# Expert stage: token rows gathered in four 1 KB pieces and turned by VectorE blocks instead of TensorE transposes

## The chip, the cores and the metric

One core of a Trainium2 chip runs the whole program. The metric is the device time of one launch in microseconds. The kernel before took 3232.83 us (median of 3 runs, 3229.73 to 3238.44).

## What is computed

Two transformer blocks over 1024 tokens of width 1024, all in fp32. The first has attention, a long convolution and a gated MLP; the second has three kinds of attention and then a mixture of experts. Only the experts are touched by the change:

```python
g_logits = x @ w_rg + b_rg                       # 4 groups
grp = argmax(g_logits)
e_logits = (x @ w_re[grp]) + b_re                # 8 experts in the group
top_val, top_idx = lax.top_k(e_logits, 2)        # 2 of 32 experts for each token
gate = softmax(top_val) * p_grp
# for each of a token's two experts e:
y_e = (silu(x @ w_gate[e]) * (x @ w_up[e])) @ w_down[e]    # 1024 -> 256 -> 1024
out[token] = sum over its two experts of gate * y_e
```

There are 1024 x 2 = 2048 pairs of token and expert.

## The kernel before

The program keeps every engine's instructions in one long stream for each engine, stage after stage. The last stages are the routing (`pe_route`, `dve_choose`, `dve_place`), the experts (`*_experts`) and the final sum and norm (`*_final`).

**Placement.** There are 32 blocks of 128 slots (NBLK), one for each expert, 4096 slots in all. Block i holds the tokens of expert i in its first slots. Slots 64 to 127 of a block form a second side with weight buffers of its own (GUEST_GU, GUEST_DN): they are first filled with a copy of the block's own weights, and an indirect load over them brings another expert's weights only where an expert has more than 128 tokens; its indices are out of bounds otherwise, and rows out of bounds are skipped. `dve_place` works out, per pair, block and slot; TensorE sums one-hot products into a table `slots` (slot in the partition, block in the column, L2677) that holds the token's number, 0 for an empty slot (constant "tok"); `widx` (L2851) holds the weight rows of the guest.

**The expert loop.** Iterations i = 0 to 33; each engine's order within one is written by hand:

- POOL (`pool_experts`, L2902 on): gathers the rows of block i+2 (L2906, 128 rows of 4 KB from the DRAM tensor `xtok` into XG, one instruction, on the software queue q0), then the guest gate/up load of block i (L2893, waits for VectorE's copy `cg`), then the guest down load of block i-1 (L2899).
- SP: on the hardware queue q1 loads the own weights of a later block (L2879, 2 MB; L2882, 1 MB) and stores the block's result (L3063, 512 KB to `yslot`).
- TensorE (`pe_experts`): `pe_ex(i)` (L2929, 8 transposes of 128x128 from XG to two PSUM banks), `pe_eht(i-2)` (L2952, 2 transposes), `pe_egu(i-1)` (L2943, 32 matmuls of 512 columns, both sides), `pe_edn(i-2)` (L2965, 16 matmuls). `pe_egu(i)` waits for XB(i), for the own weights and for the guest load ("bg", i).
- VectorE (`dve_experts`): half of block i's turned rows from PSUM to XB (L3026), hidden values of i-2 (L3031), the copy of the own gate/up weights into the guest buffer (L3013, 128x4096, gives "cg"), the product for i-1 (L3042), half of the result of i-2 (L3047); in eight iterations also a scaling (L3021).
- ScalarE: the other half of the turned rows (L2996), the copy of the down weights (L2988), silu (L3002), the other half of the result (L3007).

XG, XB, and both guest buffers are double. The stage ends with gathers of `yslot` (L3110) and the final norm.

Of the kernel before, what the change touches and what calls it, by code (L numbers as in the profile page):

```python
# [5 lines left out]
U32 = mybir.dt.uint32  # L6
ALU = mybir.AluOpType
ACT = mybir.ActivationFunctionType
# [112 lines left out]
def build(nc, X, out):  # L121
# [2462 lines left out]
    didx16 = room(16)  # L2584
    FS = marks["end"]
# [9 lines left out]
    didx = [didx16.bitcast(U32)[:, 8 * q:8 * q + 8] for q in range(2)]  # L2595
    g1f, g2f = g1.rearrange("p j u -> p (j u)"), g2.rearrange("p j u -> p (j u)")
# [59 lines left out]
    def pe_route():  # L2656
# [29 lines left out]
        held[b] = [("widx",)]  # L2686

# [95 lines left out]
    def dve_place():  # L2783
        V.wait_ge(*(yield ("cumrank",)))
# [62 lines left out]
        vt.tensor_copy(slots.bitcast(U32), bk(bank["slots"], NBLK)).then_inc(*V.step(("slots",)))  # L2847
# [3 lines left out]
        vt.tensor_copy(widx.bitcast(U32), be).then_inc(*V.step(("widx",)))  # L2851
        vt.tensor_tensor(picked, slot_e, con("bidx").rearrange("p (u e) -> p u e", u=1).broadcast_to([128, 16, 32]), MUL).then_inc(*V.step())
# [49 lines left out]
    def pool_rows(i):  # L2902
        if i > 1:
            G.wait_ge(*(yield ("ex", i - 2, 1)))
        GD.ready()
        gt.indirect_dma_start(sb(XG + i % 2 * 1024, 1024), None, x_d, by_row(slots.bitcast(U32)[:, i:i + 1])).then_inc(*GD.turn(("xg", i)))  # L2906

    def pool_experts():
        G.wait_ge(*(yield ("xk", 7, 1)))
        G.wait_ge(*(yield ("slots",)))  # L2910
        for j in range(8):
            G.wait_ge(*(yield ("xd", j)))
        yield from pool_rows(0)
        yield from pool_rows(1)
        G.wait_ge(*(yield ("widx",)))
        for i in range(NBLK + 1):
            if i + 2 < NBLK:
                yield from pool_rows(i + 2)
            if i < NBLK:
                yield from pool_guest_gu(i)  # L2920
            if i:
                yield from pool_guest_dn(i - 1)

    def pe_ex(i):
        for h2 in range(2):
            yield from claim(h2)
            P.wait_ge(*(yield ("xg", i)))
            for k in range(4):
                ins = turn(bk(h2, 128, off=k * 128), sb(XG + i % 2 * 1024 + (4 * h2 + k) * 128, 128), ident)  # L2929
            ins.then_inc(*P.step(("ex", i, h2)))  # L2930
            held[h2] = [("xb", i, h2)]

    def pe_egu(i):
        b = 2 + i % 2
        yield from claim(b)
        P.wait_ge(*(yield ("xb", i, 0)))
        P.wait_ge(*(yield ("xb", i, 1)))
# [32 lines left out]
    def pe_experts():  # L2970
        for i in range(NBLK + 2):
            if i < NBLK:
                yield from pe_ex(i)
            if i >= 2:
                yield from pe_eht(i - 2)
            if 1 <= i <= NBLK:
                yield from pe_egu(i - 1)
            if i >= 2:
                yield from pe_edn(i - 2)
# [10 lines left out]
    def act_experts():  # L2990
        for i in range(NBLK + 2):
            if i < NBLK:
                if i > 1:
                    A.wait_ge(*(yield ("egu", i - 2)))
                A.wait_ge(*(yield ("ex", i, 1)))
                st.activation(sb(XB + i % 2 * 1024 + 512, 512), bk(1), ACT.Copy).then_inc(*A.step(("xb", i, 1)))  # L2996
# [18 lines left out]
    def dve_experts():  # L3015
        for j in range(8):
            V.wait_ge(*(yield ("xd", j)))
        for i in range(NBLK + 2):
# [3 lines left out]
            if i < NBLK:  # L3022
                if i > 1:
                    V.wait_ge(*(yield ("egu", i - 2)))
                V.wait_ge(*(yield ("ex", i, 0)))
                vt.tensor_copy(sb(XB + i % 2 * 1024, 512), bk(0)).then_inc(*V.step(("xb", i, 0)))  # L3026
# [244 lines left out]
def _constants():  # L3271
# [25 lines left out]
    put("tok", 128 * np.arange(8)[None] + i[:, None])  # L3297
# [48 lines left out]
def _layout(I):  # L3346
# [19 lines left out]
    for n, s in (("qna", "qn_a"), ("kna", "kn_a"), ("qnd", "qn_d"), ("knd", "kn_d")):  # L3366
# [43 lines left out]
        wgu=np.stack([I["w_expert_gate_2"][0], I["w_expert_up_2"][0]], axis=2).reshape(32, 8, 128, 512).transpose(0, 2, 1, 3).reshape(4096, 4096),  # L3410
# [20 lines left out]
```

## Time and profile before

| | |
|---|---|
| median of 3 runs | 3232.83 us |
| the profiled execution | 3227.49 us, its span 3225.9 us |
| granted TensorE clock over the span | 0.982 of full |
| TensorE busy | 3055.8 us (95%) |
| VectorE, ScalarE, POOL busy | 1601.0, 938.6, 245.8 us |
| chain that ended last | TensorE 85%, ScalarE 7%, VectorE 6% |
| expert loop, from the first row gather to the last result stored | 2773.3 to 3167 us of the span |

A share of busy time says little about what a stage waits for: each of the stages before the routing is untouched by the change, and the expert loop has to be read by itself. "DMA share" is the mean busy share of the core's 16 DMA engines; q0 is the queue of the POOL engine's indirect transfers, q1 that of SP.

### The profile page before, as it was taken

The numbers are of one execution on the slowest core, as the hardware profiler recorded it, in microseconds if no ns is written. First come the engines' busy times: TensorE is split into PE (matmuls) and PEld (weight loads), VectorE is DVE, ScalarE is ACT, GpSimd is POOL, SyncE is SP. The second block draws the span as 40 slices with busy tenths as digits, with TensorE's granted clock in tenths as the row PEclk, the third lists the DMA queues.
The fourth block names the chain that finished last, engine by engine and source line by source line (L and its number), as shares of the span: only waits on it lengthen the run. The fifth ranks groups of instructions, "written<-read, shape, count | busy, mean of one in ns | idle before, by whom it ended". The sixth has DMA issues, their size and how long they took to land.

```text
span 3225.9 us, 30362 instructions
## 1 busy us (share of the span) xinstructions
PE 3055.8 (95%) x12214; PEld 1629.6 (51%) x12214; DVE 1601.0 (50%) x2659; ACT 938.6 (29%) x1766; POOL 245.8 (8%) x174
## 2 busy tenths in 40 slices
PE   7999999899999999999999998899999998699997
PEld 3456557566664444444444454675846643333332
DVE  6467677466653555544564422312366525443334
ACT  4112462477772100000000001212335613222223
POOL 1000231000000000000000000000000000234431
PEclk9999999999999999999999999999999999799999
DMA  6113213000003211111121020000120013599994
GB/s 244 52 65 131 79 53 118 1 1 1 1 27 132 93 49 39 51 41 40 43 90 36 27 94 27 20 30 20 50 69 1 27 52 119 185 358 358 360 336 177
DMA packets 61512, 298.19 MB, mean 92 GB/s; under 512 B 14826, under 2 KB 21242, under 8 KB 39868
## 3 DMA queue, kind: packets, MB, share of 16 engines
q1 hardware_dynamic: 45244, 271.05, 23.2%
q0 software_dynamic: 16128, 25.21, 2.2%
q8 instruction: 96, 1.57, 0.2%
q14 instruction: 44, 0.36, 0.0%
HBM read 365.32 MB, written 31.55 MB: 123 GB/s over the span
## 4 chain that ended last, share of the span: by engine, by line
PE 85%; ACT 7%; DVE 6%; issue 1%; DMA 1%; another core or an unknown queue 0%; POOL 0%; SPq 0%; DVEq 0%; ACTq 0%; POOLq 0%
PE ps L1385 16%; PE ps L1512 8%; PE ps L2943 7%; PE ps L1687 6%; PE ps L906 5%; PE ps L2965 3%; PE ps L1309 3%; PE ps L2448 3%; PE ps L1689 3%; PE ps L1059 3%; PE ps L763 3%; PE ps L909 2%; PE ps L1087 2%; PE ps L2206 2%; ACT arena L1138 2%; PE ps L1071 1%
## 5 line engine op out<-in xcount | busy, mean ns | idle before, releaser
L1385 PE MATMUL ps<-arena 128*128 128x512 f32 x1232 | 529.6, 592 | 1.0 <-DVE arena L1416 1.0
L1385 PEld LDWEIGHTS ps<-arena 128*128 128x128 f32 x1232 | 233.3, 189 | 297.3 <-issue 287.4
L1512 PE MATMUL ps<-arena 128*128 128x512 f32 x616 | 264.5, 592 | 0.0
L2943 PE MATMUL ps<-arena 128*64 128x512 f32 x1024 | 229.6, 600 | 5.2 <-DMA arena<-in_wgu_dram,arena 5.2
L1687 PE MATMUL ps<-arena 128*128 128x512 f32 x480 | 209.5, 597 | 0.0
L1193 DVE TENSOR_SCALAR_CACHE_REDUCE arena<-ps 128x1280 f32<-128x1280 f32 x96 | 139.3, 1489 | 111.9 <-PE ps L1059 111.9
L1512 PEld LDWEIGHTS ps<-arena 128*128 128x128 f32 x616 | 116.6, 189 | 147.8 <-issue 143.7
L906 PE MATMUL ps<-arena 128*128 128x512 f32 (+1 forms) x432 | 173.6, 555 | 0.7 <-DVE arena L389 0.7
L2109 POOL COPY arena<-arena 64x512 f32<-64x512 f32 x8 | 5.6, 695 | 1887.1 <-DVE arena L2102 1886.8
L1687 PEld LDWEIGHTS ps<-arena 128*128 128x128 f32 x480 | 91.0, 191 | 114.1 <-issue 114.1
L2943 PEld LDWEIGHTS ps<-arena 128*64 128x64 f32 x1024 | 73.8, 137 | 138.2 <-issue 138.2
L1704 DVE COPY arena<-ps 128x512 f32<-128x512 f32 (+2 forms) x31 | 16.6, 537 | 248.0 <-PE ps L1687 158.2
L1151 ACT ACTIVATE arena<-arena 128x1280 f32<-128x1280 f32 x96 | 129.6, 1354 | 8.2 <-DVE arena L1193 8.2
L1059 PE MATMUL ps<-arena 64*128 64x512 f32 (+1 forms) x576 | 121.0, 552 | 6.8 <-DVE arena L1193 3.1
L906 PEld LDWEIGHTS ps<-arena 128*128 128x128 f32 x432 | 82.1, 191 | 84.7 <-issue 81.4
L1071 PE MATMUL ps<-arena 128*128 128x128 f32 x640 | 100.3, 286 | 24.4 <-ACT arena L1138 21.0
L2906 POOL DMA_INDIRECT arena<-xtok,arena x32 | 82.3, 2571 | 539.6 <-DVE arena L2851 363.4
L1138 ACT ACTIVATE arena<-ps 128x512 f32<-128x512 f32 (+1 forms) x192 | 93.7, 522 | 87.0 <-PE ps L1071 84.4
L2965 PE MATMUL ps<-arena 128*64 128x512 f32 x512 | 115.7, 592 | 0.5 <-DVE arena L3031 0.5
L2448 PE MATMUL ps<-arena 128*128 128x512 f32 x256 | 111.0, 592 | 0.7 <-DVE arena L2414 0.7
L1309 PE MATMUL ps<-arena 128*128 128x512 f32 x256 | 110.4, 592 | 0.0
L1689 PE MATMUL ps<-arena 128*128 128x256 f32 (+1 forms) x512 | 104.5, 364 | 0.0
(432 smaller groups left out, 4553.8 us busy)
## 6 DMA issues: line engine op xcount, KB each, us to landing
arena<-in_wgu_dram SPq DMA_DIRECT2D x32, 2048.0 KB, 8.4
arena<-in_wed_dram SPq DMA_DIRECT2D x32, 1024.0 KB
arena<-in_wmod_dram SPq DMA_DIRECT2D x24, 1024.0 KB, 4.9
arena<-in_wup_dram SPq DMA_DIRECT2D x22, 1024.0 KB, 4.8
arena<-in_wout_dram SPq DMA_DIRECT2D x16, 1024.0 KB, 4.9
yslot<-arena SPq DMA_DIRECT2D x32, 512.0 KB, 9.6
arena<-in_wdn_dram SPq DMA_DIRECT2D x16, 704.0 KB, 4.1
arena<-in_w2b_dram SPq DMA_DIRECT2D x9, 1024.0 KB, 4.9
```

Of the source, the lines that this page charges most:

```text
L906: ins = mm(bk(b, size), sb(wat(n) + k * 256 + col, 128), x, k == 0, k == 7)
L1059: ins = mm(bk(3 * j + c // 512, n), sb(q + h * 1024 + qt * 128, 128, 64 * j, 64 * j + 64), sb(key + c, n, 64 * j, 64 * j + 64), True, True)
L1138: st.activation(probt(i, j, g * 512, n), bk(bank[("turn", i, j, g)], n), ACT.Copy).then_inc(*A.step(("pt", i, j, g)))
L1193: vt.tensor_scalar(prob(i, j), scores(j), -SCALE, None, MUL, ALU.min, accum_out=stat(i, f"bias{j}")).then_inc(*V.step(("cmax", i, j)))
L1309: ins = mm(bk(b), sb(wat(n) + k * 256 + f % 2 * 128, 128), sb(YT + k * 1024 + tc * 512, 512), k == 0, k == 7)
L1385: ins = mm(bk(b), left[:, k], right[:, k], k == 0, k == 3)
L1512: ins = mm(bk(b), sb(left + k * 128, 128), right(k), k == 0, k == 10)
L1687: ins = mm(bk(b), sb(w, 128), sb(x + tile * 512, 512), k == 0, k == 7)
L1689: ins = mm(bk(b, size), views[ty](x, tile), sb(w, size), k == 0, k == 7)
L2448: ins = mm(bk(b), sb(wat(n) + k * 256 + f % 2 * 128, 128), sb(OF + k * 1024 + tc * 512, 512), k == 0, k == 7)
L2943: ins = mm(bk(b, 512, *rows), sb(XB + i % 2 * 1024 + k * 128 + 64 * side, 64), sb(w + k * 512, 512), k == 0, k == 7)
L2965: ins = mm(bk(6 + h2, 512, *rows), sb(HB + 512 + i % 2 * 256 + k * 128 + 64 * side, 64), sb(w + k * 1024 + h2 * 512, 512), k == 0, k == 1)
```

## The change

- `slots` stays in fp32. The constant "tok" becomes 4 x token - 8192, so that an empty slot reads 0 and a full one a negative number.
- New: `quarter` (partition // 32 + 8192, four small VectorE operations, two of them a rounding), `every` (one VectorE copy, 128x512) ahead of everything in `dve_place`; four matmuls of 32 columns in `pe_route` that spread slot 32a+s to partitions s, 32+s, 64+s, 96+s; two VectorE operations that make `sidx` from them: 4 x token + quarter, or 8192 and more for an empty slot, which the bounds check skips.
- A block's rows are gathered by four indirect transfers of 128 pieces of 1 KB (partition 32b+s gets quarter b of the row of slot 32a+s) in place of one of 128 rows of 4 KB; POOL waits for `sidx` instead of `slots`, and puts the transfers in another order around the guest loads.
- `pe_ex` and its two PSUM copies (on VectorE and ScalarE) go; one VectorE transpose of 32x32 blocks, 128x1024, makes XB from XG.
- The rows of the gate/up weights are laid out in DRAM to fit, on the host.

```diff
+    sidx, quarter, every = room(4 * NBLK), room(1), room(512)
+    x_q = x_d.rearrange("t (b c) -> (t b) c", b=4)
...
+        b = next(banks)
+        yield from claim(b)
+        P.wait_ge(*(yield ("slots",)))
+        for a in range(4):
+            ins = mm(bk(b, NBLK, off=NBLK * a), every[:, 128 * a:128 * a + 128], slots, True, True)
+        bank["spread"] = b
+        ins.then_inc(*P.step(("spread",)))
+        held[b] = [("sidx",)]
...
     def dve_place():
+        vt.tensor_scalar(quarter, con("pidx"), 1 / 32, -31 / 64, MUL, ADD).then_inc(*V.step())
+        vt.tensor_copy(every.rearrange("p (a b s) -> p a b s", a=4, b=4),
+                       ident.rearrange("p (a u s) -> p a u s", a=4, u=1).broadcast_to([128, 4, 4, 32])).then_inc(*V.step(("every",)))
+        dve_round(quarter)
+        vt.tensor_scalar(quarter, quarter, 8192.0, None, ADD).then_inc(*V.step())
         V.wait_ge(*(yield ("cumrank",)))
...
-        vt.tensor_copy(slots.bitcast(U32), bk(bank["slots"], NBLK)).then_inc(*V.step(("slots",)))
+        vt.tensor_copy(slots, bk(bank["slots"], NBLK)).then_inc(*V.step(("slots",)))
...
         vt.tensor_copy(widx.bitcast(U32), be).then_inc(*V.step(("widx",)))
+        V.wait_ge(*(yield ("spread",)))
+        vt.tensor_scalar(sidx, bk(bank["spread"], 4 * NBLK), quarter, None, ADD).then_inc(*V.step())
+        vdone()
+        vt.tensor_copy(sidx.bitcast(U32), sidx).then_inc(*V.step(("sidx",)))
...
-    def pool_rows(i):
+    def pool_rows(i, quarters):
         if i > 1:
-            G.wait_ge(*(yield ("ex", i - 2, 1)))
-        GD.ready()
-        gt.indirect_dma_start(sb(XG + i % 2 * 1024, 1024), None, x_d, by_row(slots.bitcast(U32)[:, i:i + 1])).then_inc(*GD.turn(("xg", i)))
+            G.wait_ge(*(yield ("xb", i - 2)))
+        for a in quarters:
+            GD.ready()
+            gt.indirect_dma_start(sb(XG + i % 2 * 1024 + a * 256, 256), None, x_q, by_row(sidx.bitcast(U32)[:, NBLK * a + i:NBLK * a + i + 1]),
+                                  bounds_check=4095, oob_is_err=False).then_inc(*GD.turn(("xg", i, a)))
...
-        yield from pool_rows(0)
-        yield from pool_rows(1)
         G.wait_ge(*(yield ("widx",)))
+        G.wait_ge(*(yield ("sidx",)))
+        yield from pool_rows(0, (0, 1, 2, 3))
+        yield from pool_guest_gu(0)
+        yield from pool_rows(1, (0, 1, 2, 3))
         for i in range(NBLK + 1):
             if i + 2 < NBLK:
-                yield from pool_rows(i + 2)
-            if i < NBLK:
+                yield from pool_rows(i + 2, (0, 1))
+            if 0 < i < NBLK:
                 yield from pool_guest_gu(i)
+            if i + 2 < NBLK:
+                yield from pool_rows(i + 2, (2, 3))
             if i:
                 yield from pool_guest_dn(i - 1)
...
-        P.wait_ge(*(yield ("xb", i, 0)))
-        P.wait_ge(*(yield ("xb", i, 1)))
+        P.wait_ge(*(yield ("xb", i)))
...
                 if i > 1:
                     V.wait_ge(*(yield ("egu", i - 2)))
-                V.wait_ge(*(yield ("ex", i, 0)))
-                vt.tensor_copy(sb(XB + i % 2 * 1024, 512), bk(0)).then_inc(*V.step(("xb", i, 0)))
+                for a in range(4):
+                    V.wait_ge(*(yield ("xg", i, a)))
+                vt.transpose(sb(XB + i % 2 * 1024, 1024).rearrange("p (k a s) -> p a k s", k=8, a=4),
+                             sb(XG + i % 2 * 1024, 1024).rearrange("p (a k s) -> p a k s", k=8, a=4)).then_inc(*V.step(("xb", i)))
...
-    put("tok", 128 * np.arange(8)[None] + i[:, None])
+    put("tok", 4 * (128 * np.arange(8)[None] + i[:, None]) - 8192)
...
-        wgu=np.stack([I["w_expert_gate_2"][0], I["w_expert_up_2"][0]], axis=2).reshape(32, 8, 128, 512).transpose(0, 2, 1, 3).reshape(4096, 4096),
+        wgu=np.stack([I["w_expert_gate_2"][0], I["w_expert_up_2"][0]], axis=2).reshape(32, 4, 8, 32, 512).transpose(0, 1, 3, 2, 4).reshape(4096, 4096),
```

## Rows read from the trace of the kernel before

**Rows 1.** The page's busy times: engine, us, share, instructions.
```profile
PE 3055.8 (95%) x12214; PEld 1629.6 (51%) x12214; DVE 1601.0 (50%) x2659; ACT 938.6 (29%) x1766; POOL 245.8 (8%) x174
```

**Rows 2.** The chain of waits: start us, us, what; its first blocks and last one.
```profile
2773.30 4.80 DMA arena<-xtok,arena
...
2783.41 3.80 DMA arena<-in_wgu_dram,arena
...
2787.35 9.36 PE ps L2943 x32
...
2798.14 7.03 PE ps L2943 x32
...
2809.85 7.03 PE ps L2943 x32
2816.89 3.43 PE ps L2965 x16
2820.32 1.02 PE ps L2929 x8
...
3148.23 0.37 PE ps L2952 x2
3148.60 7.03 PE ps L2943 x32
3155.63 3.43 PE ps L2965 x16
```

**Rows 3.** Stretches: us, busy of PE, PEld, DVE, ACT, POOL, PEclk, DMA share, GB/s.
```profile
2787.00:2789.00 2.00, 1.65 (x4) 0.59 (x6) 0.00 (x0) 0.00 (x0) 1.39 (x3) 0.50 0.45 104
2820.93:2832.64 11.71, 11.71 (x60) 4.64 (x59) 5.00 (x6) 3.40 (x5) 4.71 (x3) 1.00 1.01 362
```

**Rows 4.** Timeline of VectorE in one block: start us, us, what, [idle before].
```profile
2818.65 0.69 DVE L3047 COPY arena<-ps 128x512 f32<-128x512 f32 x1 [0.87 <-PE ps L2965]
...
2820.95 0.69 DVE L3026 COPY arena<-ps 128x512 f32<-128x512 f32 x1 [1.00 <-PE ps L2929]
2821.60 0.42 DVE L3031 COPY arena<-ps 128x256 f32<-128x256 f32 x1
2821.94 2.28 DVE L3013 COPY arena<-arena 128x4096 f32<-128x4096 f32 x1
```

**Rows 5.** VectorE by line, 2763 to 2767 us: one-pass operation, 1024 elements, both sides SBUF.
```profile
L2835 DVE TENSOR_TENSOR arena<-arena 128x1024 f32<-128x1024 f32 x2 | 2.4, 1218 | 0.0
```

**Rows 6.** Timeline of POOL: the first two gathers, then one block's three issues.
```profile
2773.30 1.59 POOL L2906 DMA_INDIRECT arena<-xtok,arena  x1 [363.42 <-DVE arena L2851]
2775.19 0.94 POOL L2906 DMA_INDIRECT arena<-xtok,arena  x1 [0.30 <-issue]
...
2821.62 2.73 POOL L2906 DMA_INDIRECT arena<-xtok,arena  x1 [6.03 <-PE ps L2952]
2825.02 0.99 POOL L2893 DMA_INDIRECT arena<-in_wgu_dram,arena  x1 [0.67 <-issue]
2826.31 0.99 POOL L2899 DMA_INDIRECT arena<-in_wed_dram,arena  x1 [0.31 <-issue]
```

**Rows 7.** POOL by line, 2773 to 3160 us: xcount, busy us, mean ns, idle before.
```profile
L2906 POOL DMA_INDIRECT arena<-xtok,arena x32 | 82.3, 2571 | 539.6 <-DVE arena L2851 363.4 <-PE ps L2952 162.8 <-PE ps L2929 12.8
```

**Rows 8.** TensorE by line, 2765 to 2773 us: the 16 matmuls of 32 columns.
```profile
L2677 PE MATMUL ps<-arena 128*128 128x32 f32 x32 | 7.0, 401 | 9.6 <-DVE arena L2835 9.6
```

**Rows 9.** Timeline of VectorE in the routing: a wait, the slots, the guests' rows.
```profile
2755.66 0.19 DVE L2786 TENSOR_SCALAR arena<-ps 128x32 f32<-128x32 f32 x1 [0.93 <-PE ps L2670]
...
2772.26 0.19 DVE L2847 CAST arena<-ps 128x32 uint32<-128x32 f32 x1 [4.62 <-PE ps L2677]
```

**Rows 10.** Line L2893, the guest gate/up load, all 32: from issue to landing.
```profile
DMA to landing us min/median/max: 6.1/6.7/7.4
```

**Rows 11.** DMA queues, 2859.6 to 2862.8 us: packets, MB, share.
```profile
q1 hardware_dynamic: 155, 0.94, 96.9%
```

**Rows 12.** DMA queues, 2863.4 to 2865.4 us.
```profile
q0 software_dynamic: 338, 0.45, 61.1%
q1 hardware_dynamic: 58, 0.32, 60.2%
```

**Rows 13.** DMA queues, 3176 to 3185 us: gathers of 4 KB rows alone.
```profile
DMA packets 976, 3.55 MB, mean 395 GB/s; under 512 B 109, under 2 KB 109, under 8 KB 976
```

**Rows 14.** DMA queues, 2344.5 to 2350.3 us: a load of 1,056-byte rows alone.
```profile
DMA packets 1950, 2.04 MB, mean 352 GB/s; under 512 B 16, under 2 KB 1950, under 8 KB 1950
```

**Rows 15.** DMA queues, 2786.5 to 2787.8 us: the first guest load, all rows skipped.
```profile
q0 software_dynamic: 144, 0.00, 4.9%
```

More of the change, by code:

```diff
@@ L2900, in pool_guest_dn @@
                               bounds_check=4095, oob_is_err=False).then_inc(*GD.turn(("bd", i)))
-    def pool_rows(i):
+    def pool_rows(i, quarters):
         if i > 1:
-            G.wait_ge(*(yield ("ex", i - 2, 1)))
-        GD.ready()
-        gt.indirect_dma_start(sb(XG + i % 2 * 1024, 1024), None, x_d, by_row(slots.bitcast(U32)[:, i:i + 1])).then_inc(*GD.turn(("xg", i)))
+            G.wait_ge(*(yield ("xb", i - 2)))
[3 more added lines that the diff above has]
+                                  bounds_check=4095, oob_is_err=False).then_inc(*GD.turn(("xg", i, a)))
     def pool_experts():
         G.wait_ge(*(yield ("xk", 7, 1)))
-        G.wait_ge(*(yield ("slots",)))
         for j in range(8):
             G.wait_ge(*(yield ("xd", j)))
-        yield from pool_rows(0)
-        yield from pool_rows(1)
         G.wait_ge(*(yield ("widx",)))
+        G.wait_ge(*(yield ("sidx",)))
+        yield from pool_rows(0, (0, 1, 2, 3))
+        yield from pool_guest_gu(0)
+        yield from pool_rows(1, (0, 1, 2, 3))
         for i in range(NBLK + 1):
             if i + 2 < NBLK:
-                yield from pool_rows(i + 2)
-            if i < NBLK:
+                yield from pool_rows(i + 2, (0, 1))
+            if 0 < i < NBLK:
                 yield from pool_guest_gu(i)
+            if i + 2 < NBLK:
+                yield from pool_rows(i + 2, (2, 3))
             if i:
                 yield from pool_guest_dn(i - 1)
[L2924 to L2931, printed above, removed]
     def pe_egu(i):
@@ L2971, in pe_experts @@
         for i in range(NBLK + 2):
-            if i < NBLK:
-                yield from pe_ex(i)
             if i >= 2:
@@ L2991, in act_experts @@
         for i in range(NBLK + 2):
[L2992 to L2996, printed above, removed]
             if 1 <= i <= NBLK:
```

## The prediction

> **What bounds the kernel now.** I read the page's busy times first: TensorE is busy for 95% of the span [rows 1], and the change takes work off it, in the expert loop alone. So the second view is the chain of waits over that loop [rows 2]. It is a strict pattern: down matmuls 3.43 us, the transposes of the gathered rows 1.02 us, two short transposes, gate/up matmuls 7.03 us, from one start at 2809.85 us to the last at 3148.60 us. TensorE waits for nothing in between; the period is 11.71 us. The stretch of one period [rows 3] shows the second thing: the DMA engines are busy too, 362 GB/s at a share of 1.01. TensorE sets the pace, and the transfers just keep up. The start is different: chain pieces of 4.80 and 3.80 us are DMA landings [rows 2], one after the other.
>
> **TensorE, per block.** Removed: the 8 transposes, 1.02 us on the path. The last iteration has none of them and shows the period that would remain: 0.37 + 7.03 + 3.43 = 10.83 us [rows 2]. That is 0.88 us less than 11.71 (the two short transposes then hide less). This is the floor.
>
> **VectorE and ScalarE.** The two PSUM copies go (0.69 us on VectorE [rows 4], about as much on ScalarE, which is far from full). The block transpose has no row. Nearest is a one-source-rate operation over 1024 elements, 1.22 us [rows 5]; lower bound the 2.28 us for 4096 elements [rows 4] scaled to 1024, 0.6; upper bound twice the first, 2.4. I take 1.22, the row nearest in elements and in operands. VectorE goes from 5.00 us a period [rows 3] to 5.5 of 10.8: no bound. It also no longer needs TensorE: it may start when the result copy ends, 0.98 us before TensorE's iteration starts (2819.34 against 2820.32 [rows 2, 4]), and ends at +0.24 us.
>
> **POOL, per block.** Six issues in place of three. A free issue takes 0.94 to 0.99 us and 0.30 to the next [rows 6]. The mean of the row gathers is 2.57 us [rows 7], but the one that starts at 2821.62 ends at 2824.35, 0.13 us after VectorE's big copy (2821.94 to 2824.22 [rows 4]): it stands still under the copy. The copy comes once a block, so I charge that stall once. From TensorE's iteration start: gather 0 from 0.4 to 3.3 (the copy now ends at 3.1), gather 1 3.6 to 4.6, guest load issued at 4.9, gathers 2 and 3 to 8.5, down load to 9.8. It fits into 10.8 with 1 us to spare. Twelve semaphore waits more for the transfers in flight (they take their turns among 16) wait for landings two blocks old: free.
>
> **The guest load decides.** It moves nothing (all rows skipped), but gate/up of block i waits for it. Before, it is issued at +4.70 (2825.02) and lands 6.7 us later [rows 6, 10], at +11.4, needed at +12.95: 1.5 us early. Now it is issued at +4.9 and needed at 10.83 + 0.37 = +11.2. With the same 6.7 us it lands at +11.6, 0.4 late, which makes the period 11.23. But what lies ahead of it shrinks. While q1 had work, q0 moved nothing [rows 11], and once q1 ran dry q0 moved its 0.5 MB [rows 12]: the queues are served about in order of arrival. Ahead of it in q0 are now two gathers of at most 0.26 MB instead of 0.52. At 395 GB/s for 4 KB rows [rows 13] and 352 for 1,056-byte ones [rows 14] that is 0.75 us instead of 1.33: landing at +11.0, just in time. The landings vary by 0.6 to 0.7 us [rows 10], so some come late: I take 10.93 us for the period (ends 10.83 and 11.4).
>
> **Bytes.** 2048 pairs fill half of 4096 slots, so the loop moves 3.93 MB a block on the average instead of 4.19; 256 more skipped pieces cost little: 144 packets took 4.9% of 1.3 us [rows 15], 0.06 us, so 0.12. DMA work falls by 1.33 - 0.75 - 0.12, some 0.45 us a period (0.26 MB at 285 to 395 GB/s gives 0.92 to 0.66).
>
> The trace has 395 GB/s out of HBM over 9 us [rows 13], so I do not take the loop's 362 for a ceiling. The Trainium skill (DMA: Bandwidth & Descriptors, Where 436 GB/s comes from) says that loads from HBM are bound at about 358 GB/s for a core. By that, as an estimate, 3.93 MB give a period of 10.98 us, 1.5 us more over the loop than mine; the gathers' rate speaks against it here.
>
> **The routing.** New work ahead of the wait for the counts: five VectorE operations, about 1.2 us (0.2 each, the 512-element copy 0.4), of which 0.93 lie in a wait that is there [rows 9]: +0.3. The spread: 8 passes at 7.0/32 = 0.22 us [rows 8], 1.75 us, with two small VectorE operations and the handovers: gathers start at about 2775.8 instead of 2773.3, +2.5 us.
>
> **The start of the loop.** Four gathers instead of one before block 0 can be turned: the fourth is issued by 2781.1 and has landed by 2783.1; transpose to 2784.3, copy to 2786.6, guest load issued 2786.9, landed 1.1 us after its end: gate/up of block 0 at 2789.1 instead of 2787.35. It runs on a cold clock as before (0.50 granted, 1.2 GHz [rows 3], 9.36 us instead of 7.03 [rows 2]) and ends at 2798.5. Then POOL's queue is in the way: between the guest loads of blocks 0 and 1 stand ten gathers (four of block 1, four of 2, two of 3), 10 x 1.25 us and one stall under a copy: issued about 2802.8 instead of 2787.65. The own load of block 3, issued at 2798.5, lies ahead in the DMA engines until about 2805. So gate/up of block 1 starts at about 2806.5 instead of 2798.14, after 8 us of idle TensorE, likely with the clock at its lower level again: 9.4 us. Block 2 starts at about 2820 instead of 2809.85: **+10 us** for the start as a whole (bounds +3, if POOL's issues overlap better, and +13). Cover that is gone: before, block 1's guest load went out 10 us ahead of need.
>
> **Sum.** From 2809.85 to 3148.60 are 338.75 us. Now 29 periods x 10.93 = 317.0: -21.8. With the start, +10: **-12 us**. The tail is unchanged. Profiled execution 3227.49 (span 3225.9), so about 3215.5; the median of the runs shown is 5 us above that execution, so I say 3221 for the median.
>
> **Rivals.**
> - *A late guest load each block.* Its landing time stays at 6.9 us or the transfers do not get cheaper: 4.9 + 6.9 - 0.37 = 11.4 us a period, 29 x 11.4 = 330.6, -8 + 10 = +2: 3235. For it: 1.5 us of margin before, and the change takes 0.88 of it by speed alone. Against: half the bytes.
> - *POOL becomes the bound (the slower end).* If each row gather takes 2.57 us wherever it stands [rows 7]: 4 x 2.57 + 1.04 + 0.99 + 6 x 0.30 = 14.1 us a period, 29 x 2.4 = +70, +10: 3313. It decides from 1.5 us per issue on (6 x 1.8 = 10.8). Against: 0.94 and 0.99 where no copy runs [rows 6]. A milder form is a second stall of 1.7 us a block, which only just goes over: 11.9 a period, +15: 3248.
> - *Small pieces choke the transfers.* The Trainium skill (DMA: Bandwidth & Descriptors, Measured) warns that transfers under 64 KB are descriptor-dominated; the gathers shrink from 512 to 128 KB. On the rows, 1,056-byte packets run at 352 GB/s when many are queued [rows 14]; for this to cost, 0.26 MB would have to take longer than 1.8 us. It would end in the same place as the first rival.
> - *The start costs little:* +3, period 10.83: 314.1 - 338.75 + 3 = -22: 3211.
> - *The empty slots are not skipped:* 8192 and more is over the bound 4095, so no; it would be the first rival.
>
> **Chances.** Forecast 0.52, late guest load or dearer transfers 0.27, POOL 0.11, cheap start 0.10. 0.3% is 9.7 us, about what a measurement can tell from no change: faster means below 3223. My forecast lies only 2 us under that, so of its 0.52 I count 0.37 as faster. Faster 0.47, same 0.40, slower 0.13. The range takes in the cheap start with the runs' spread of some 4 us and the late guest load: 3206 to 3240.
>
> **What would show it.** Right: chain pieces 0.37, 7.03, 3.43 without L2929, a period of 10.8 to 11.1; POOL with one long gather and three of 1 us; a VectorE transpose of 1.2 us; block 2's gate/up at about 2820. Wrong: chain pieces "DMA in_wgu" or POOL in every block (late guest load, POOL), POOL busy over 10 us a period, a first period start before 2813, or a DMA share under 0.9.

## The result, and the profile after

The changed kernel takes **3251.37 us** (median of 4 runs, 3249.51 to 3252.67) against 3232.11 for the kernel before beside it: a ratio of 1.0051, 95% interval 1.0032 to 1.0069. It is slower by about 19 us (the two medians alone give 1.0060), where I had forecast 12 us less and a range of 3206 to 3240. The profiled execution is one of 3249.51 us.

The page of the changed kernel: the span, busy times, DMA queues, the chain's shares, and three of its groups of instructions (two matmul lines of the experts and the row gathers).

```profile
span 3248.2 us, 30137 instructions
PE 3039.5 (94%) x11966; PEld 1609.0 (50%) x11966; DVE 1617.2 (50%) x2666; ACT 919.3 (28%) x1734; POOL 343.9 (11%) x270
q1 hardware_dynamic: 45244, 271.05, 23.2%
q0 software_dynamic: 17664, 16.86, 1.6%
PE 77%; DVE 7%; ACT 7%; DMA 4%; issue 3%; POOL 1%; another core or an unknown queue 0%; POOLq 0%; DVEq 0%; SPq 0%; ACTq 0%
L2957 PE MATMUL ps<-arena 128*64 128x512 f32 x1024 | 232.1, 605 | 26.1 <-DMA arena<-in_wgu_dram,arena 26.1
L2926 POOL DMA_INDIRECT arena<-xtok,arena x128 | 181.6, 1419 | 465.5 <-DVE arena L2871 366.6
L2979 PE MATMUL ps<-arena 128*64 128x512 f32 x512 | 116.6, 594 | 22.1 <-DMA arena<-in_wed_dram,arena 19.1
```

TensorE's gate/up matmuls (L2957) now stand idle 26.1 us for the guest gate/up load, its down matmuls (L2979) 22.1 us, 19.1 of them for the guest down load. Both loads carry nothing here: all their rows are skipped. Of before, the chain had the first only ahead of block 0 [rows 2], and the second nowhere.

Most of the 26.1 us lie at the start of the loop, ahead of blocks 0 and 1:

```profile
2794.07 10.09 PE L2957 MATMUL ps<-arena 128*64 128x512 f32 x32 [15.15 <-DMA arena<-in_wgu_dram,arena]
2813.50 8.91 PE L2957 MATMUL ps<-arena 128*64 128x512 f32 x32 [7.91 <-DMA arena<-in_wgu_dram,arena]
```

Behind them, in the 29 periods up to block 31, TensorE waits for the gate/up load twice, 3.0 us in all, and for the down load fifteen times, 19.1 us in all. In the steady loop it is the down load that is late. Who waited for its line, L2918 (us, times):

```profile
  PE ps L2979: 19.1, 15
```

The chain of waits, two neighbouring blocks (columns: start us, us, what):

```profile
2835.26 10.68 DMA arena<-in_wed_dram,arena
2845.94 0.14 issue
2846.08 3.65 PE ps L2979 x16
2849.73 0.37 PE ps L2966 x2
2850.10 7.05 PE ps L2957 x32
...
2866.40 10.11 DMA arena<-in_wgu_dram,arena
2876.51 0.14 issue
2876.65 3.62 PE ps L2957 x15
```

The matmul pieces are those of the forecast (0.37, 7.05 us; the down matmuls take 3.65 us behind a wait and 3.43 without one); between them stand landings of 10.68 us (down load) and 10.11 us (gate/up load). Wherever the chain of these periods shows a late down load, it landed 9.1 to 10.9 us after its issue. Before, the guest gate/up load landed after 6.1 to 7.4 us [rows 10], the guest down load after 2.1 to 6.2 us, with a median of 5.5. The gate/up matmuls of blocks 2 to 31 start from 2826.1 to 3169.3 us, 29 periods of 10.83 to 15.8 us with a mean of **11.83** (the expectations below round it to 11.84); before, a constant 11.71 (the last one shorter), which makes a mean of 11.68.

GpSimd in one block (start us, us, what):

```profile
2851.27 2.60 POOL L2926 DMA_INDIRECT arena<-xtok,arena  x1 [3.37 <-DVE arena L3040]
2854.18 1.00 POOL L2926 DMA_INDIRECT arena<-xtok,arena  x1 [0.30 <-issue]
2855.48 0.99 POOL L2912 DMA_INDIRECT arena<-in_wgu_dram,arena  x1 [0.30 <-issue]
2856.77 1.00 POOL L2926 DMA_INDIRECT arena<-xtok,arena  x1 [0.30 <-issue]
2858.08 1.00 POOL L2926 DMA_INDIRECT arena<-xtok,arena  x1 [0.30 <-issue]
2859.38 1.00 POOL L2918 DMA_INDIRECT arena<-in_wed_dram,arena  x1 [0.30 <-issue]
```

One issue stretched under VectorE's copy, five of 1.00 us: as worked out, and GpSimd is done 9.1 us after it began. But it begins later than worked out. Counted from the start of TensorE's two short transposes (2849.73 here), the guest gate/up load is issued at +5.6 us in the median block instead of +4.9, and the guest down load at +9.5; before, the down load was issued at +6.0, counted from the start of the eight transposes.

VectorE's block transpose, the new operation (line, operation, shapes, count, busy us, mean ns, idle before):

```profile
L3034 DVE STREAM_TRANSPOSE arena<-arena 128x1024 f32<-128x1024 f32 x32 | 39.6, 1237 | 21.5 <-DMA arena<-xtok,arena 21.5
```

**Where the 22.3 us between the two spans lie.** 4.3 lie ahead of the routing's matmuls, which start at 2769.5 instead of 2765.2. I take them for drift: of the change only a few small VectorE operations stand there, and the first gather of kernels that are alike up to it starts anywhere from 2775.2 to 2780.6. From there to the first gather 11.04 instead of 8.09: +2.95. First gather to block 2's gate/up 45.6 instead of 36.5: +9.1. The 29 periods: 343.2 instead of 338.75, +4.4. The tail: +1.5.

### The profile page after: what moved, and what is told of

Same layout as the page of the kernel before. It is cut to its first block, busy times and chain, and to the rows that moved or that the text cites. A ratio compares the mean times of both kernels' runs of the same rounds, so it can differ in the third digit from the quotient of the medians.

```text
span 3248.2 us, 30137 instructions
## 1 busy us (share of the span) xinstructions
PE 3039.5 (94%) x11966; PEld 1609.0 (50%) x11966; DVE 1617.2 (50%) x2666; ACT 919.3 (28%) x1734; POOL 343.9 (11%) x270
## 3 DMA queue, kind: packets, MB, share of 16 engines
q0 software_dynamic: 17664, 16.86, 1.6%
## 4 chain that ended last, share of the span: by engine, by line
PE 77%; DVE 7%; ACT 7%; DMA 4%; issue 3%; POOL 1%; another core or an unknown queue 0%; POOLq 0%; DVEq 0%; SPq 0%; ACTq 0%
PE ps L1385 16%; PE ps L1512 8%; PE ps L1687 6%; PE ps L906 5%; PE ps L1309 3%; PE ps L2448 3%; PE ps L1689 3%; DMA arena<-in_wed_dram,arena 3%; PE ps L1059 3%; PE ps L763 3%; PE ps L909 2%; PE ps L2957 2%; PE ps L2979 2%; PE ps L1087 2%; ACT arena L1138 2%
## 5 line engine op out<-in xcount | busy, mean ns | idle before, releaser
L2957 PE MATMUL ps<-arena 128*64 128x512 f32 x1024 | 232.1, 605 | 26.1 <-DMA arena<-in_wgu_dram,arena 26.1
L2926 POOL DMA_INDIRECT arena<-xtok,arena x128 | 181.6, 1419 | 465.5 <-DVE arena L2871 366.6
L2957 PEld LDWEIGHTS ps<-arena 128*64 128x64 f32 x1024 | 75.6, 139 | 159.9 <-issue 159.9
L2979 PE MATMUL ps<-arena 128*64 128x512 f32 x512 | 116.6, 594 | 22.1 <-DMA arena<-in_wed_dram,arena 19.1
```

Of the source, the lines that this page charges most:

```text
L2926: gt.indirect_dma_start(sb(XG + i % 2 * 1024 + a * 256, 256), None, x_q, by_row(sidx.bitcast(U32)[:, NBLK * a + i:NBLK * a + i + 1]), boun ...
L2957: ins = mm(bk(b, 512, *rows), sb(XB + i % 2 * 1024 + k * 128 + 64 * side, 64), sb(w + k * 512, 512), k == 0, k == 7)
L2979: ins = mm(bk(6 + h2, 512, *rows), sb(HB + 512 + i % 2 * 256 + k * 128 + 64 * side, 64), sb(w + k * 1024 + h2 * 512, 512), k == 0, k == 1)
```

## The experiments

All times are medians; the ratio is to the kernel before on the same chip, and the quotient of the two medians differs from it by up to 0.0015; the mean period is that of blocks 2 to 31 in the profiled run.

| kernel | us | ratio (95%) | mean period |
|---|---|---|---|
| changed | 3251.4 | 1.0051 (1.0032 to 1.0069) | 11.83 |
| no_guest_loads | 3206.1 | 0.9916 (0.9895 to 0.9937) | 10.84 |
| one_gather | 3279.2 | 1.0125 (1.0091 to 1.0159) | 13.85 |
| one_gather_hold | 3288.4 | 1.0155 (1.0122 to 1.0188) | 13.71 |
| loads_first_loop | 3237.5 | 1.0011 (0.9993 to 1.0028) | 11.52 |
| after_small_own | 3232.8 | 0.9994 (0.9984 to 1.0005) | 11.27 |
| after_empty_fetched | 3249.3 | 1.0048 (1.0031 to 1.0064) | 11.96 |
| early_copy | 3209.9 | 0.9917 (0.9889 to 0.9945) | 10.84 |
| early_copy_start | 3216.0 | 0.9941 (0.9920 to 0.9962) | 10.85 |
| before_skipped_more | 3239.1 | 1.0020 (1.0002 to 1.0038) | 11.88 |
| before_empty_skipped | 3235.8 | 1.0002 (0.9987 to 1.0018) | 11.68 |
| before_early_copy | 3229.2 | 0.9987 (0.9977 to 0.9996) | 11.68 |
| before_four_pieces | 3348.4 | 1.0344 (1.0312 to 1.0376) | 15.34 |
| before_four_skipped | 3360.5 | 1.0391 (1.0366 to 1.0417) | 15.88 |
| before_four_split | 3249.8 | 1.0039 (1.0020 to 1.0057) | 12.16 |

### 1. Without the guest loads

```
-        yield from pool_guest_gu(0)
...
-            if 0 < i < NBLK:
-                yield from pool_guest_gu(i)
...
-            if i:
-                yield from pool_guest_dn(i - 1)
```

> The changed kernel with both guest loads of every block left out (with these inputs they skip every row; their place is taken by VectorE's and ScalarE's copies, on which TensorE now waits). Turns theory: the last transfers of queue q0 land late because every piece, skipped ones too, takes a turn with q1's packets, and the guest loads are what TensorE waits for: without them the period falls from 11.84 to 10.83 us, 29 periods give back some 29 us against the changed kernel, the start a little more: about 0.5% faster than before, near 3215 us. Rival, transfers at their ceiling: the small pieces cost the DMA engines more than the empty slots save, the own weights come late, and the period stays at 11.8: +15 us against before. Rival, POOL or VectorE too slow: the period stays above 11.5.

Both guest loads are left out (the copies stay, and with these inputs nothing is loaded by them). Measured: 3206.1 us, and a period of 10.83 to 10.84 in every block. The chain (start us, us, what):

```profile
2885.77 0.37 PE ps L2959 x2
2886.14 7.03 PE ps L2950 x32
2893.17 3.44 PE ps L2972 x16
```

So the forecast's floor is real, and the loss in the periods goes with the two loads that move nothing. The start is cheap too: block 2 at 2810.2.

### 2. One gather of whole rows, and guest loads first

```
-        for a in quarters:
+        if quarters[0] == 0:
...
-            gt.indirect_dma_start(sb(XG + i % 2 * 1024 + a * 256, 256), None, x_q, ...
+            gt.indirect_dma_start(sb(XG + i % 2 * 1024, 1024), None, x_d, ...
```

> The changed kernel with one gather of whole 4 KB rows for each block in place of the four (empty slots still skipped), and the same VectorE transpose; the rows then do not lie in quarters, so what is computed from them is another product of the same size. Turns theory: q0 holds 24 pieces a block for each engine instead of 48, the guest loads land as early as before, period 10.83 to 10.95 us, and the start loses only 3 to 5 us: 3212 us, 0.6% faster than before. Rival, the VectorE transpose or the order of the loop is what costs: period as in the changed kernel, 11.8, 3245 us.

The rows lie in another layout than the block transposes want. The expectation has the empty slots still skipped; in effect they are not. The one column of indices that it uses holds slots 0 to 31 four times over, which are nearly always full, and q0 moves 25.11 MB in all, against 16.86 in the changed kernel and 25.21 in the one before. So it compares four gathers of the full slots with one gather of as many bytes as before. Measured: 3279.2 us, slower still, where I had expected 3212. Fewer issues do not cure it. Here it is the guest gate/up load that is late: TensorE waits for it in 14 of the 29 periods, 54.6 us in all, though it is issued at +4.3 us. GpSimd here issues all the rows, then both guest loads. In the next kernel they come in the reverse order:

```
         for i in range(NBLK + 1):
+            if i:
+                yield from pool_guest_dn(i - 1)
+            if 0 < i < NBLK:
+                yield from pool_guest_gu(i)
             if i + 2 < NBLK:
-                yield from pool_rows(i + 2, (0, 1))
+                yield from pool_rows(i + 2, (0, 1, 2, 3))
```

> The changed kernel with POOL's order in the loop turned round: guest down load, guest gate/up load, then the four gathers of block i+2. Nothing else. Turns theory: the guest loads no longer have the block's 16 to 32 pieces an engine ahead of them, they land 4 us or more earlier, TensorE does not wait, period 10.85 to 11.1; the start stays as in the changed kernel (+12 us against before): 3222 to 3230 us. Rival, transfers at their ceiling: the same bytes and pieces, so no change from the changed kernel, 3250 us.

Measured: 3237.5 us, between the expectation (3222 to 3230) and its rival (3250). The down load, now issued first, at +3.3 us, is waited for in no period; the gate/up load in five, 12.0 us in all. Across the three kernels the period falls with what stands ahead of the guest loads: all rows 13.85 us, half of them 11.83, none 11.52. The first of the three also differs in the form and the bytes of its gather, so the order alone is shown only by the other two.

> The kernel before with one more indirect transfer in each block, 128 pieces that are all out of bounds and skipped, issued just ahead of the guest gate/up load. It moves nothing. Turns theory: 8 more pieces in each engine's q0, each waiting for a packet of q1 of up to 16 KB (0.4 to 0.7 us), so the guest load lands 3 to 5 us later than now, 2 to 3.5 us past the 1.5 us of margin: period 13 to 15 us, 3270 to 3330 us. Rival, order of arrival (the prediction's reading): a skipped piece costs 7 ns, the issue moves 1.3 us, which the margin covers: no change, 3230 to 3235 us.

This one puts a gather of 128 pieces that are all skipped ahead of the guest gate/up load in the kernel before. Measured: 3239.1 us, a period of 11.71 but for two blocks (15.67 and 13.41, with one guest landing of 11.1 us). The turns theory, which had 13 to 15 us a period, fell here: in nearly every block the 128 skipped pieces cost nothing, as the rival had it (the median landing is 5.8 us, from an issue 0.9 us later). The one late block shows that the kernel before stands close to an edge.

### 3. What the two queues do

Ahead of the next experiments I read the DMA queues in stretches (packets, MB, share of the 16 engines). The kernel before, 2857 to 2862.5 us, then 2863.5 to 2866:

```profile
q1 hardware_dynamic: 219, 1.82, 95.9%
...
q1 hardware_dynamic: 54, 0.36, 53.1%
q0 software_dynamic: 380, 0.47, 51.3%
```

The gather issued from 2856.75 on (its issue on GpSimd ends at 2859.48) gets nothing up to 2862.5, with two own loads and the store of the results issued before it; then q1 is nearly dry and q0 does most of its block's work, 380 packets, in 2.5 us. The next own gate/up load is issued at 2863.76, and when its large packets move, from about 2866 on, q0 is almost through. The changed kernel, inside the landing of 10.11 us, 2872 to 2874 us, then 2874 to 2876:

```profile
q1 hardware_dynamic: 49, 0.80, 98.1%
q0 software_dynamic: 39, 0.00, 1.2%
...
q1 hardware_dynamic: 56, 0.59, 89.1%
q0 software_dynamic: 168, 0.00, 4.9%
```

In the first stretch q1 is at its 2 MB load with packets of 16 KB (0.80 MB in 49), and q0's packets, skipped pieces without bytes, go between them nearly one for one: 39 in 2 us, where 380 took 2.5 us above. From this I took it that taking turns with large packets makes the 10 us of an empty load. In the second stretch q0 moves three packets for each of q1's. The Trainium skill (DMA: Bandwidth & Descriptors, Queues, rings and completion order) says that each engine goes round-robin between its queues, packet by packet; the first stretch agrees (39 to 49), the stretch of before in which q0 had nothing does not. The profile adds up 16 engines, so no stretch shows the turns of one of them.

Another reading is the order of issue. SyncE issues the own gate/up load at 2868.01 and GpSimd the guest down load at 2870.30, behind it; before, the down load was issued at 2861.44, ahead of the own load at 2863.76.

I first took it that the own load issued too early catches q0's tail, and held it back:

```
                 S.wait_ge(*(yield ("egu", i - 1)))
+                S.wait_ge(*(yield ("bg", i)))
                 sp_own_gu(i + 2)
```

> The kernel with one gather of 4 KB rows and VectorE's transposes, with one wait added on SyncE: it does not issue the own gate/up load of block i+2 until the guest gate/up weights of block i have landed. Theory (the last skipped pieces of the other queue are caught behind 16 KB packets of the next own load when that load is issued before they are done): the landing of 12 to 14 us disappears (none over 9), the periods of 15 to 19 us too, and the mean falls from 13.9 to 11.5 or less; the time 3205 to 3245. Rival (the guest loads are late whatever is queued behind them, since the skipped pieces themselves take the time): landings stay at 12 to 14 us, now with the own load late behind them, mean 14 to 16, the time 3280 to 3340.

Measured: 3288.4 us, and the expectation fell. The guest loads still land after 11.5 and 12.7 us (medians; 7.8 and 6.6 without the wait), because the held load is now always issued with the next block's gathers. 2983 to 2987 us:

```profile
q1 hardware_dynamic: 84, 1.38, 80.8%
q0 software_dynamic: 74, 0.30, 19.0%
```

Again nearly one for one, 74 to 84, with 16 KB (1.38 MB in 84) on the other side. Holding the own load does not help. Against the theory stands the kernel without the wait, one_gather, inside a landing of 12.31 us, 2990 to 2995 us:

```profile
q1 hardware_dynamic: 158, 1.97, 97.3%
q0 software_dynamic: 16, 0.01, 0.6%
```

This would still be turns if only one or two engines had packets of q0 left, which the sums over 16 engines do not show. If a guest packet waits for one packet of 16 KB, half the packet should mean half the wait. The next test halves it:

```
-        dma.dma_start(out=sb(OWN_GU[i % 3], 4096), in_=X["wgu"][128 * i:128 * i + 128, :]).then_inc(gusem[i % 3], 16)
+        for c in (0, 2048):
+            dma.dma_start(out=sb(OWN_GU[i % 3] + c, 2048), in_=X["wgu"][...]).then_inc(gusem[i % 3], 16)
```

> The changed kernel with one edit on the other queue: each own gate/up load (2 MB) is issued as two loads of 1 MB, so that its packets are 8 KB instead of 16 KB; the bytes, the order on GpSimd and all the waits stay. Theory (on each DMA engine the packets of the two queues go in turn, one and one, so a piece of the guest queue waits for one packet of the own queue, and the wait is the size of that packet): the guest queue drains up to twice as fast beside the gate/up load, the mean period falls from 11.84 to 10.9 to 11.5, the time to 3215 to 3238. Rival 1 (the guest loads are late because the queues are served in order of arrival, or because the engines' work is too much): nothing changes, 3245 to 3256. Rival 2 (the second issue or the smaller packets cost the own load its rate): slower, over 3256.

Measured: 3232.8 us, the mean period 11.27 instead of 11.83, with no change to the bytes or to what is waited for. In its chain a late gate/up load now lands after 7.02 us, and late down loads after 9.0 to 9.9 us instead of 9.1 to 10.9:

```profile
2836.78 7.02 DMA arena<-in_wgu_dram,arena
2843.80 0.14 issue
2843.94 7.11 PE ps L2958 x32
```

The theory's range held this one; both rivals had said 3245 or more. Of the 22.8 us between the two profiled executions the 29 periods give 16.4; block 2 starts at 2820.5 instead of 2826.1, of which 5.3 is drift before the first gather. The edit halves the packet and also makes two transfers of one, and no run parts these.

### 4. TensorE's pace or the traffic

```
-            gt.indirect_dma_start(sb(XG + i % 2 * 1024, 1024), None, x_d, ...
+            gt.indirect_dma_start(sb(XG + i % 2 * 1024 + a * 256, 256), None, x_q, ...   (a = 0 to 3)
```

> The kernel before, with its one gather of 4 KB rows per block replaced by four gathers of 1 KB pieces to the same places; all rows, the empty ones too, are fetched, and the 32 turns stay on TensorE. Theory (TensorE's 11.71 us period leaves the other queue room, and it is only the shorter period that takes it away): period 11.71 in most blocks, a few later ones, the start of the loop 2 to 3 us later for the three more issues on GpSimd, the time 3234 to 3245. Rival (small pieces cost the DMA engines so much that the loop is bound by them): every period over 12, the time over 3245.

> The kernel before with four gathers of 1 KB pieces instead of one of 4 KB rows, empty slots skipped, and TensorE's turns kept: the changed kernel's data movement at the TensorE period of before. With all pieces fetched this came to a mean period of 15.8 and 3348 us. Theory (fetched 1 KB pieces hold the guest queue up, skipped ones hardly): mean period 11.71 to 12.3, some blocks of 13 and over, the time 3233 to 3255. Rival (the number of packets in the guest queue alone decides, whatever they carry, and that is the same as with all pieces fetched): mean period over 14, the time over 3300.

The second has the same edit with the empty slots skipped. Measured: 3348.4 and 3360.5 us. I had expected some 3240 and 3233 to 3255; the rivals won both. Skipping did not help at all. The cause is GpSimd's queue, which I had left out: all four gathers stand ahead of the guest gate/up load. GpSimd in the second (start us, us, what):

```profile
2884.18 1.00 POOL L2909 DMA_INDIRECT arena<-xtok,arena  x1 [0.30 <-issue]
2885.49 1.00 POOL L2909 DMA_INDIRECT arena<-xtok,arena  x1 [0.30 <-issue]
2886.79 0.99 POOL L2909 DMA_INDIRECT arena<-xtok,arena  x1 [0.31 <-issue]
2888.09 1.00 POOL L2895 DMA_INDIRECT arena<-in_wgu_dram,arena  x1 [0.30 <-issue]
2889.39 0.99 POOL L2901 DMA_INDIRECT arena<-in_wed_dram,arena  x1 [0.30 <-issue]
```

Three more issues of 1.30 us put the load 3.9 us later, where [rows 10] and its need left 1.5 us. That alone does not make waits of 5 to 8 us: its late landings are 8.9 to 11.4 us as well. To part this from the traffic, the same kernel with the changed kernel's order on GpSimd:

```
             if i + 2 < NBLK:
-                yield from pool_rows(i + 2)
+                yield from pool_rows(i + 2, (0, 1))
             if i < NBLK:
                 yield from pool_guest_gu(i)
+            if i + 2 < NBLK:
+                yield from pool_rows(i + 2, (2, 3))
```

> The kernel before with four gathers of 1 KB pieces, empty slots skipped, TensorE's turns kept, and now GpSimd's order of the changed kernel (two gathers, guest gate/up load, two gathers, guest down load), so that the guest load is issued 1.3 us later than before instead of 3.9 us. It is the changed kernel but for who transposes. Theory (the shorter TensorE period takes away the room in which the guest queue is served): period 11.71 in most blocks (mean under 12.0), start up to 10 us later, the time 3233 to 3250. Rival (the four-piece traffic and its issues on GpSimd are enough to make the guest loads late): mean period 12.3 or more, the time 3255 or more.

Measured: 3249.8 us, mean period 12.16, between the two ranges (under 12.0 and over 12.3). Even at TensorE's old pace the new traffic makes guest loads late, here the down load:

```profile
2876.15 10.03 DMA arena<-in_wed_dram,arena
2886.18 0.29 issue
2886.47 3.65 PE ps L2972 x16
2890.13 1.03 PE ps L2936 x8
```

So both halves count: the four gathers cost 12.16 - 11.68 = 0.48 us a block, and TensorE's saving of 0.88 then brings only 12.16 - 11.83 = 0.33. The 0.48 is not traffic alone: the down load is here issued some 4 us later than before, behind the gathers on GpSimd, and it lands after 10 us instead of 5.5. Before, it had 7.6 us to spare (issued at 2826.31, landed 6.2 us later at most, needed at 2840.1), which only the two together use up.

> The changed kernel with the empty slots' pieces fetched (from row 0 of the tokens) instead of skipped: four gathers of 1 KB pieces, 512 fetched pieces per block. Theory (each fetched packet of four 1 KB pieces takes 0.24 us against 0.16 us for a 4 KB row, and stands in front of the guest loads): the mean period rises from 11.84 to 13 to 16, the time to 3280 to 3360. Rival (skipping is worth only its 0.25 MB per block of transfer, 0.6 to 1 us of the engines' work): mean period 12.4 to 12.9, the time 3265 to 3280.

Edit: the constant 8192 that sends empty slots over the bound becomes 0, in `quarter` and in "tok". Measured: 3249.3 us, as the changed kernel. Expectation and rival (3265 to 3280) both fell: 8.35 MB more, and nothing to see.

> The kernel before, with nothing changed but that rows of empty slots are skipped by the gathers. It moves about 8 MB less in the loop, with the period set by TensorE at 11.71. Theory (TensorE sets the period and less work for the DMA engines buys nothing at 11.71): 3228 to 3237, within 0.2% of before. Rival (the DMA engines' work is part of the bound already): period 11.4 to 11.6, the time 3222 to 3229. Other rival (skipped pieces hold the queue up, as in the kernel with one gather and VectorE's transposes): several periods of 13 to 15, the time 3240 to 3260.

The reverse, in the kernel before: 3235.8 us, ratio 1.0002, period 11.71 in every block but the last. Skipping is worth nothing either way. So it is not the bytes of the gathers that count; the order on GpSimd (loads_first_loop) and the packets of the other queue (after_small_own) do.

### 5. More room for the guest load

VectorE's copy of the guest gate/up weights, and with it the load, one block earlier, and the guest down load first in GpSimd's order:

```
+        yield from pool_rows(1, (0, 1, 2, 3))
         yield from pool_guest_gu(0)
-        yield from pool_rows(1, (0, 1, 2, 3))
...
+        yield from pool_guest_gu(1)
+        yield from pool_rows(2, (0, 1, 2, 3))
+        for i in range(1, NBLK + 1):
+            yield from pool_guest_dn(i - 1)
+            if i + 2 < NBLK:
+                yield from pool_rows(i + 2, (0, 1, 2, 3))
+            if i + 1 < NBLK:
+                yield from pool_guest_gu(i + 1)
...
-            if i < NBLK:
-                yield from dve_guest_gu(i)
+            if i == 0:
+                yield from dve_guest_gu(0)
...
                 vt.tensor_tensor(h, h, ..., MUL).then_inc(*V.step(("eh", i - 1)))
+            if i + 1 < NBLK:
+                yield from dve_guest_gu(i + 1)
```

> The changed kernel with VectorE's copy of the guest gate/up weights moved one block earlier, and the guest gate/up load issued a whole block ahead of its use: on GpSimd the order per block is guest down load (i-1), the four gathers of rows (i+2), guest gate/up load (i+1). Theory (the guest loads have no slack, the own loads have some 7 us): the guest gate/up weights may now land up to 8 us later than before without TensorE waiting, so the period falls from a mean of 11.84 towards 10.83 with only the down load left to be late now and then (mean 10.9 to 11.3), and the time to 3205 to 3235. Rival 1 (the DMA engines' work per block is itself about 11.8 us with these small pieces): the period stays at 11.6 to 11.9 and the time at 3245 to 3255. Rival 2 (it is the guest down load alone that is late): the period is irregular as before, with waits on the down load of 1 to 4 us, the time 3240 to 3255.

Measured: **3209.9 us**, 0.9917 of the kernel before (0.9889 to 0.9945), with the whole computation, all six issues and both loads in. The period is 10.83 to 10.84 but for one of 10.95. The down load is issued at +3.3 us instead of +9.5, and the gate/up load at +0.9 us for the block after, so both have gained room. With the down load first alone (loads_first_loop) the period was 11.52. The chain, and one period of it (us, busy us of PE, PEld, DVE, ACT, POOL, then the granted clock, DMA share, GB/s):

```profile
2881.11 7.04 PE ps L2956 x32
2888.15 3.43 PE ps L2978 x16
2891.58 0.37 PE ps L2965 x2
```

```profile
3000.40:3011.24 10.84, 10.84 (x53) 3.79 (x52) 4.69 (x6) 2.79 (x4) 7.90 (x7) 1.00 1.00 376
```

TensorE is busy through the period, and the DMA engines are at a share of 1.00 with 376 GB/s: both are full, neither waits. Rival 1 (the small pieces are too much work for the engines) is refuted by the period.

> The kernel before, with only the order of the kernel called early_copy: VectorE's guest gate/up copy and the guest gate/up load one block earlier. TensorE keeps its turns. It tells whether the 25 us that early_copy gained over the kernel before come from the new order alone. Theory (TensorE's 11.71 us of work set the period, and the order only matters once that is gone): period 11.71, the time 3225 to 3240, within 0.3% of before. Rival (the order alone is worth it): period under 11.5, the time under 3222.

The same order in the kernel before: 3229.2 us, 0.9987, period 11.71. The order alone brings 3 us; the change alone costs 19; both together gain 25. TensorE's work was the bound before, and taking it off only shows once the guest loads have room.

> The kernel called early_copy with another order at the start alone: GpSimd issues the guest gate/up load of block 0 after two gathers of block 1 instead of four, and VectorE's copy for block 1 comes after the transpose of block 1, so that it does not stall the issue of block 0's load. Theory (that load is what block 0's gate/up waits for): gate/up of block 0 starts 2 to 3 us earlier, the period stays at 10.83, the time 3205 to 3208. Rival (the loss moves to block 1, whose rows or load then come late): within 1 us of early_copy, 3209 to 3212.

Edit: at the start `pool_rows(1, (0, 1))`, guest load 0, `pool_rows(1, (2, 3))`, and VectorE's copy for block 1 after that block's transpose. Measured: 3216.0 us, 6 more than early_copy. Block 0 does start earlier (2790.0 instead of 2794.9), but block 2 waits for its guest load and starts at 2817.9 instead of 2816.0. The loss moved, as the rival said, and grew beyond its range (3209 to 3212). The profiled execution is the fastest of six, which go up to 3220.9.

## Why the prediction was wrong

- **TensorE's floor, 10.83 us:** right, shown by no_guest_loads and early_copy.
- **VectorE's transpose, 1.22 us:** 1.24 us, the mean of the 32 above. Right.
- **POOL's six issues in 10.8 us, one stall:** right for the sum (9.1 us). But the first gather starts at +1.0 us where TensorE doesn't wait, not at +0.4, and its issue takes 3.0 us: the guest gate/up load is issued at +5.6 us instead of +4.9.
- **The guest down load: no term in the sum.** This is the step that cost most in the periods. The forecast has its issue ("down load to 9.8"), but neither a landing nor a need, and names no cover. It is issued at +9.5 us and needed at 10.83 + 0.37 + 7.03 = +18.2, so it may take 8.7 us; with the 5.5 us of before it would have been in time. It took 9.1 to 10.9 us where the chain shows it. Of the 29.1 us that the 29 periods stand above the floor (343.2 - 314.1), TensorE is idle 19.1 for this load, in fifteen periods, and 3.0 for the gate/up load, in two.
- **"The queues are served about in order of arrival":** the second step that failed. It was read from two stretches [rows 11, 12] in which the two queues happened to have their work apart, and it gave +11.0 us for the gate/up load's landing. In the changed kernel packets of both queues go side by side, and the empty load shown above took 10.1 us instead of 6.7. Halving the other queue's packets shortened the period by 0.56 us, which order of arrival doesn't explain. That the guest loads take turns with the own loads is the best account of these runs, but not the only one: before_skipped_more and the stretch of one_gather speak against its simple form. I forecast 10.93 us a period; 11.83 came.
- **Bytes, -0.45 us a period:** worth nothing in either kernel (after_empty_fetched, before_empty_skipped).
- **No ceiling at 362 GB/s:** right, early_copy moves 376. My estimate of 10.98 us from the Trainium skill's 358 GB/s (DMA: Bandwidth & Descriptors, Where 436 GB/s comes from) set it against 3.93 MB, among them the store of 0.52 MB, which is no load. early_copy's period is 10.84 us, and its 376 GB/s are over that figure with the store in them, but its loads alone are not (4.08 MB less 0.52 in 10.84 us is 328). The gathers alone ran over it [rows 13], and there the measurement decides.
- **Routing +2.5 us to the first gather:** +2.95. **Start as a whole +10:** +12.1 (2.95 + 9.1), and for the reason given: the guest gate/up loads of blocks 0 and 1.
- **Sum:** forecast -21.8 + 10. Measured +4.4 + 12.1 + 1.5 of tail. Against the profiled execution I had said 3215.5; it was 3249.5, 34.0 more: 26.2 from the periods, 2.1 from the start, 1.5 from the tail, 4.3 from the drift ahead of the routing, which makes 34.1 (the forecast had rounded -11.8 to -12).

The first rival (a late guest load each block, 11.4 us, 3235) was the nearest in kind, but it meant the gate/up load, and its price of 0.47 us a block over my 10.93 was too small: 0.90 came, mostly from the load that it doesn't name. The milder POOL rival gave 3248 by another mechanism, a second stall, which did not occur. A chance of 0.13 for slower was too low for a loop with two loads needed at a fixed time, of which I had priced one.

**What stays open.** Why q0 gets nothing in one stretch, one packet for each of q1's in another, and three in the next isn't settled. Nor is it how much of the down load's late landing comes from its new place behind the own load of 2 MB, and how much from turns with its packets. It was not tried either what makes the late blocks come at irregular distances.

## What to carry to other kernels

A transfer that is empty still has its landing time, and here that moved between some 6 and 13 us with the order of issue and the packets of the other queue, not with the bytes of the gathers. Before taking work off the engine that sets the period, or putting issues ahead of a load, list each load that is needed a fixed time after its issue, and its margin under the new order; here the one that was left off the list cost most. If a margin is small, first issue that load earlier. Here the two edits brought -3 and +19 us alone, and -25 together.

## What the hardware showed that I had not expected

- Two DMA queues with work at the same time moved 39 to 49 and 74 to 84 packets in two stretches, nearly one for one, but also 168 to 56 and 16 to 158 in two others. Packets of no bytes went at 39 in 2 us beside 16 KB packets and at 380 (with 0.47 MB) in 2.5 us beside a queue nearly dry.
- Splitting the large load in two, with packets of 8 instead of 16 KB, took 0.56 us off the mean period.
- Fetching or skipping half of the gathered pieces made no difference to the time, in the kernel before and in the changed one.
